# HGRN2 recurrence with the keys' logarithm in the exponents, and a new order of work at the head boundary

## The reference

```python
def hg_dir(p, z, lb):
    q = jax.nn.silu(to_heads(p[4], HG_HEADS))
    f = lbh + (1.0 - lbh) * jax.nn.sigmoid(to_heads(z, HG_HEADS).astype(jnp.float32))
    return q, 1.0 - f, to_heads(p[7], HG_HEADS), jnp.log(f)
...
b = jnp.cumsum(la, axis=2)
scores = jnp.einsum('bhtsd,bhsd->bhts', qc[:, :, :, None, :] * decay, kc)
new_state = (jnp.exp(b_end[:, :, 0, :])[..., None] * state
             + jnp.einsum('bhsd,bhsv->bhdv', kc * jnp.exp(b_end - b), vc))
```

## Time and profile before

| | |
|---|---|
| median of three runs | 2730.33 us |
| the profiled execution's own time, its span | 2731.74 us, 2729.8 us |
| PE, DVE, ACT, POOL busy over the span | 2571.3, 2054.5, 1455.5, 542.8 us |
| mean granted clock of TensorE | 0.975 of full |
| PE busy in 262 to 296 us (boundary after head 0) | 22.8 of 34 us |
| PE busy in 424 to 467 us (boundary after head 2) | 25.9 of 43 us |
| PE busy in 513 to 2730 us (all later stages) | 2121.7 of 2217 us |

### The profile page before, as it was taken

How to read it: one execution, slowest core, us unless ns; L and a number is a source line. 1 busy time by engine, 2 the same in 40 slices (tenths; PEclk the granted TensorE clock), 3 DMA queues, 4 the chain that set the end, 5 groups by cost and what they waited for, 6 DMA issues and landing times.

```text
span 2729.8 us, 45966 instructions
## 1 busy us (share of the span) xinstructions
PE 2571.3 (94%) x16329; PEld 2201.9 (81%) x16330; DVE 2054.5 (75%) x2515; ACT 1455.5 (53%) x1648; POOL 542.8 (20%) x423
## 2 busy tenths in 40 slices
PE   7998987999897999999999999999999999999995
PEld 3896766777886788877887979899989897898885
DVE  5437788545677896999879788766686778968786
ACT  5446665213443664777647565644454456645554
POOL 0035565200023211122121111111111212112111
PEclk9999988999997999999999999999999999999998
DMA  7121111442244996999969788766586678968793
GB/s 290 39 88 37 30 42 57 160 165 93 89 88 133 346 380 212 382 358 356 318 234 364 266 300 278 272 224 208 191 304 209 236 262 313 354 206 293 266 318 134
DMA packets 274965, 607.07 MB, mean 222 GB/s; under 512 B 21837, under 2 KB 52981, under 8 KB 273761
## 3 DMA queue, kind: packets, MB, share of 16 engines
q1 hardware_dynamic: 254496, 562.41, 57.7%
q0 software_dynamic: 20384, 43.51, 7.0%
HBM read 582.87 MB, written 46.97 MB: 231 GB/s over the span
## 4 chain that ended last, share of the span: by engine, by line
PE 36%; issue 11%; DVE 9%; ACT 5%; DMA 4%; SPq 1%; DVEq 1%; POOL 1%; ACTq 0%; POOLq 0%
PE e_acc L2609 7%; PE e_acc L2612 7%; PE e_acc L2610 7%; PE e_acc L2582 4%; PE e_acc L2584 4%; PE e_acc L2583 4%; DVE e_slot_r L2765 3%; ACT whi L2693 3%; DMA list_now<-lists 3%; SPq L2341 1%; PE e_tb L2551 1%; DVE yo L2851 1%; DVE e_alo L2774 1%; DVE e_glu L2827 1%; DMA slot<-in_w 1%
## 5 line engine op out<-in xcount | busy, mean ns | idle before, releaser
L2693 ACT ACTIVATE whi<-e_slot 128x2048 fp32r<-128x2048 f32 x296 | 561.5, 1914 | 395.2 <-PE e_acc L2612 327.0
L2765 DVE TENSOR_TENSOR e_slot_r<-e_slot,whi 128x2048 fp32r<-128x2048 f32 x296 | 674.9, 2287 | 114.2 <-ACT whi L2693 114.2
L2609 PE MATMUL e_acc<-e_xhi,whi 128*128 128x256 f32 x1664 | 398.9, 282 | 4.5 <-ACT e_xhi L2697 4.5
L2693 ACT ACTIVATE whi<-slot 128x2048 fp32r<-128x2048 f32 x148 | 283.2, 1913 | 180.5 <-PE e_acc L2584 180.2
L2765 DVE TENSOR_TENSOR slot_r<-slot,whi 128x2048 fp32r<-128x2048 f32 x151 | 344.3, 2282 | 24.4 <-ACT whi L2693 21.8
L2582 PE MATMUL e_acc<-whi,e_ahi 128*128 128x512 f32 x800 | 320.3, 400 | 4.3 <-DVE e_glu L2827 4.3
L2609 PEld LDWEIGHTS e_acc<-e_xhi,whi 128*128 128x128 f32 x1664 | 313.2, 188 | 7.6 <-ACT e_xhi L2697 7.6
L2584 PE MATMUL e_acc<-whi,e_alo 128*128 128x512 f32 x800 | 313.3, 392 | 0.0
L2583 PE MATMUL e_acc<-e_slot_r,e_ahi 128*128 128x512 f32 x800 | 311.4, 389 | 0.0
L2509 POOL DMA_INDIRECT sum<-yo,e_idx_now x48 | 118.5, 2470 | 949.7 <-issue 505.9
L2582 PE MATMUL e_acc<-whi,e_xhi 128*128 128x512 f32 x768 | 304.4, 396 | 1.3 <-DVE e_slot_r L2765 1.1
(11 more groups left out here) (449 smaller groups left out, 4993.3 us busy)
## 6 DMA issues: line engine op xcount, KB each, us to landing
e_slot<-in_w SPq DMA_DIRECT2D x296, 1024.0 KB, 7.6
slot<-in_w SPq DMA_DIRECT2D x151, 1024.0 KB
rv<-in_w_ada SPq DMA_DIRECT2D x32, 512.0 KB, 5.4
slot<-in_w_in SPq DMA_DIRECT2D x9, 1024.0 KB, 9.7
wa<-in_w_ada SPq DMA_DIRECT2D x8, 1024.0 KB, 17.1
slot<-in_w_in SPq DMA_DIRECT2D x12, 512.0 KB, 4.4
xt<-in_x SPq DMA_DIRECT2D x8, 512.0 KB, 14.8
slot<-in_w_out SPq DMA_DIRECT2D x4, 1024.0 KB, 14.2
```

Source lines behind the costliest of these rows:

```text
L2609: pe.matmul(out[:, c, :], whi[i % RING][:, w], xhi[:, kk, :], start=first, stop=False, skip_group_check=True)
L2693: act.activation(whi[i % RING][:], raw[i % PIECES][:], ACT.Copy).then_inc(S["whi_made"], 1)
L2765: v.tensor_tensor(wlo[i % PIECES][:], raw[i % PIECES][:], whi[i % RING][:].bitcast(F32), ALU.subtract).then_inc(S["wlo_made"], 1)
```

## The change

The keys enter as logarithms. ACT takes the sigmoid of `-z`, so that `keyA`, `keyB` hold the key without its factor; `gate_logs` has the gate as one minus factor times that; `key_logs` then turns them in place into the key's logarithm, and DVE's `keys` adds or subtracts the running sums. After that an exponential alone yields the decayed key (`key_decays`) and the key side of every level, so `decayed_keys` and the two key multiplications per level are gone. `sum_keys` forms the plain sum of both directions' keys before the logarithm, into `key_sum`.

POOL makes the same 24 differences for each half, in another order: six query and six key ones of the forward direction, `roots` of the head before between, then twelve of the backward direction.

At the boundary PE has the two gate groups of head `h + 2` behind the first transpose group. The transposes use `h_tb`, and only group 4 uses `h_po` (`turn_bank`); the next head's transposed keys are copied by DVE instead of ACT (head 0's still by ACT). On DVE the copies follow `finish`, the backward scans stand behind `keys(h + 1, 0)`, and the decayed queries are made last.

```diff
...
-        scan = t.sb("h_scan", [P, HN])
+        scan = t.sb("h_scan", [P, PAIR])
+        key_sum = t.sb("h_key_sum", [P, SEQ])
...
-        wk = t.sb("h_wk", [P, NL + 1, HN])
+        wk = t.sb("h_wk", [P, NL, HN])
...
+        def turn_bank(n):
+
+            return tb[n == 4]
+
...
             def turn_keys(h, n):
                 d, g = divmod(n, 3)
-                pe.wait_ge(S["dec_ready"], 6 * h + 2 * d + 2)
+                pe.wait_ge(S["kdec_ready"], 2 * h + d + 1)
                 if n == 0:
                     pe.wait_ge(S["states"], 2 * (LT + 1) * h)
-                if n == 1:
+                if n == 4:
                     pe.wait_ge(S["o_ready"], LT * h)
-                pe.wait_ge(S["ktok_ready"], 6 * h + max(0, n - 1))
+                pe.wait_ge(S["ktok_ready"], 6 * h + (0, 1, 2, 3, 3, 4)[n])
                 for i in range(min(4, NT - 4 * g)):
                     c = 4 * g + i
-                    tt = pe.transpose(tb[n % 2][:, i * P:(i + 1) * P], kdec[d][:, c * P:(c + 1) * P], ident[:])
+                    tt = pe.transpose(turn_bank(n)[:, i * P:(i + 1) * P], kdec[d][:, c * P:(c + 1) * P], ident[:])
...
-                    pe.wait_ge(S["ktok_ready"], 6 * h + n + 1)
+                    pe.wait_ge(S["ktok_ready"], 6 * h + (6 if n == 4 else n + 1))
...
+                    pe.wait_ge(S["key_sums"], 2 * h + half + 1)
+                    pe.wait_ge(S["lev_exp"], 2 * NL * (2 * h + half + 1))
                     pe.wait_ge(S["lev_ready"], 2 * h + half + 1)
-                pe.matmul(out[:, 0:P], wk[:, NL, i * P:(i + 1) * P], q[:, j * P:(j + 1) * P], start=True, stop=True)
+                pe.matmul(out[:, 0:P], key_sum[:, j * P:(j + 1) * P], q[:, j * P:(j + 1) * P], start=True, stop=True)
...
                     for n in range(6):
                         turn_keys(h + 1, n)
+                        if n == 0 and h + 2 < HEADS:
+                            gates_of_keys(h + 2, 0)
+                            gates_of_keys(h + 2, 1)
                     updates(h + 1)
-                    if h + 2 < HEADS:
-                        gates_of_keys(h + 2, 0)
-                        gates_of_keys(h + 2, 1)
-                    else:
+                    if h + 2 == HEADS:
                         for x in range(EARLY_FIRST):
                             early_rows(x)
...
-            def logs(h):
+            def key_sigmoids(h):
                 for d in range(2):
                     act.wait_ge(S["z_copied"], 6 * h + 3 * d + 3)
                     for x, _ in key_pieces(h, d):
-                        act.activation(x, x, ACT.Sigmoid).then_inc(S["z_sig"], 1)
+                        act.activation(x, x, ACT.Sigmoid, scale=-1.0).then_inc(S["z_sig"], 1)
+
...
-                        act.activation(ahead[:, :, 1:STEP] if d else to, tiles(x) if d else x, ACT.Ln, scale=bound[:, h, d, 1:2], bias=bound[:, h, d, 0:1]).then_inc(S["logf"], 1)
-
...
+                        act.activation(ahead[:, :, 1:STEP] if d else to, tiles(x) if d else x, ACT.Ln, scale=bound[:, h, d, 2:3], bias=offset[:, 0:1]).then_inc(S["logf"], 1)
+
+            def key_logs(h, half):
+                act.wait_ge(S["key_sums"], 2 * h + half + 1)
+                act.wait_ge(S["logf"], 4 * h + 4)
+                for d in range(2):
+                    x = key_pieces(h, d)[half][0]
+                    act.activation(x, x, ACT.Ln, scale=bound[:, h, d, 1:2], bias=offset[:, 1:2]).then_inc(S["key_logs"], 1)
+
+            def key_decays(h, d):
+                act.wait_ge(S["keys_ready"], 4 * h + 2 * d + 2)
+                if d:
+                    act.wait_ge(S["gate_part"], h)
+                    act.wait_ge(S["turned"], 6 * h)
+                    for x, part in key_pieces(h, 1):
+                        k = act.activation(kdec[1][:, part], x, ACT.Exp)
+                else:
+                    act.wait_ge(S["u_done"], 6 * h)
+                    for (x, part), (cum, _) in zip(key_pieces(h, 0), cum_pieces(h)):
+                        for i, to in enumerate(range(part.start, part.stop, P)):
+                            k = act.activation(kdec[0][:, to:to + P], tiles(x)[:, i], ACT.Exp, bias=tiles(cum)[:, i, P - 1:P])
+                k.then_inc(S["kdec_ready"], 1)
...
-                        first_level(h, half)
+                        first_level(h, half, "queries")
+                        first_level(h, half, "keys")
                         continue
-                    act.wait_ge(S["lev_sub"], DIFF * h + half * DIFF // 2 + 4 * l)
-                    for x in (wk, wq):
+                    done = DIFF * h + half * DIFF // 2 + 2 * (NL - 1) + 2 * l
+                    for x, n in ((wq, done - 1), (wk, done)):
+                        act.wait_ge(S["lev_sub"], n)
                         act.activation(x[:, l, :], x[:, l, :], ACT.Exp).then_inc(S["lev_exp"], 1)
...
-                    logs(h + 1)
-                    key_decays(h + 1)
+                    key_sigmoids(h + 1)
+                    gate_logs(h + 1)
+                    key_logs(h + 1, 0)
+                    if h + 2 < HEADS:
+                        high_chunk(3 * h + 6)
+                    key_logs(h + 1, 1)
                     query_sig(h + 1, 0)
+                    key_decays(h + 1, 0)
                 elif EARLY > EARLY_FIRST + 3:
                     early_rows(EARLY - 1)
                 roots(h, 1)
                 if more:
                     query_sig(h + 1, 1)
-                    if h + 2 < HEADS:
-                        high_chunk(3 * h + 6)
-                    query_decays(h + 1)
+                    first_level(h + 1, 0, "queries")
+                    key_decays(h + 1, 1)
+                    first_level(h + 1, 0, "keys")
                     totals(h + 1)
-                    for n in range(6):
-                        turned_keys(h + 1, n)
-                        levels(h + 1, 0, ((), (0,), (), (1,), (), (2,))[n])
+                    levels(h + 1, 0, range(1, 4))
                     if h + 2 == HEADS:
                         high_early(0)
                         high_early(1)
-                    levels(h + 1, 0, range(3, NL))
+                    levels(h + 1, 0, range(4, NL))
+                    query_decays(h + 1)
                     gate_sig(h + 1)
...
+                    if of == "q":
+                        out, x, y, op = (q4[:, :, :, 0], mb, bwd[:, :, :, 0], ALU.subtract) if d else (q4[:, :, :, 1], fwd[:, :, :, 1], mf, ALU.subtract)
+                    else:
+                        out, x, y, op = (k4[:, :, :, 1], k1[:, :, :, 1], mb, ALU.subtract) if d else (k4[:, :, :, 0], k0[:, :, :, 0], mf, ALU.add)
+                    g.tensor_tensor(out, x, y, op).then_inc(S["lev_sub"], 1)
+
+                g.wait_ge(S["cumulated"], 6 * h + 3)
+                for l in range(1, NL):
+                    difference(l, "q", 0)
+                g.wait_ge(S["keys_ready"], 4 * h + 2)
+                for l in range(1, NL):
+                    difference(l, "k", 0)
+                if roots_of is not None:
+                    roots(roots_of, 1)
+                g.wait_ge(S["cumulated"], 6 * h + 6)
+                for l in range(1, NL):
+                    difference(l, "q", 1)
+                    if l == 1:
+                        g.wait_ge(S["keys_ready"], 4 * h + 4)
+                    difference(l, "k", 1)
...
+            def sum_keys(h, half):
+                v.wait_ge(S["z_sig"], 4 * h + 4)
+                if h:
+                    v.wait_ge(S["s_done"], LT * (h - 1) + (half + 1) * HT)
+                to = key_sum[:, half * HN:(half + 1) * HN]
+                k0, k1 = (latent_key(h, d, half) for d in range(2))
+                v.tensor_scalar(to, k0, bound[:, h, 0, 1:2], None, ALU.mult).then_inc(S["summed"], 1)
+                v.wait_ge(S["summed"], 2 * h + half + 1)
+                v.scalar_tensor_tensor(to, k1, bound[:, h, 1, 1:2], to, ALU.mult, ALU.add).then_inc(S["key_sums"], 1)
+
             def keys(h, d):
-                v.wait_ge(S["logf"], 4 * h + 2 * d + 2)
-                for x, _ in key_pieces(h, d):
-                    v.tensor_scalar(x, x, bound[:, h, d, 2:3], bound[:, h, d, 1:2], ALU.mult, ALU.add).then_inc(S["keys_ready"], 1)
+                v.wait_ge(S["cumulated"], 6 * h + 3 * d + 3)
+                for half, (x, _) in enumerate(key_pieces(h, d)):
+                    v.wait_ge(S["key_logs"], 4 * h + 2 * half + d + 1)
+                    if d:
+                        k = v.tensor_tensor(tiles(x), tiles(x), ahead_pieces(h)[half][0][:, :, 0:P], ALU.add)
+                    else:
+                        k = v.tensor_tensor(x, x, cum_pieces(h)[half][0], ALU.subtract)
+                    k.then_inc(S["keys_ready"], 1)
...
             def level(h, half, l):
-                lo, hl = half * HN, LEVELS[l]
...
+                lo = half * HN
                 if l == 0:
...
-                    v.tensor_tensor(wk[:, NL, :], k0, k1, ALU.add).then_inc(S["lev_sum"], 1)
...
```

(54 more changed lines are left out.)

128 lines of the change are left out of this document (60 added, 68 removed).

## The result

The changed kernel takes 2738.66 us (median of eight runs, 2734.72 to 2741.99) against 2730.0 us of the kernel before in the same measurement: ratio 1.003, interval 1.0021 to 1.0039. It is slower by 8.7 us, where 8.5 us of gain were forecast. Its profiled execution has a span of 2737.5 us against 2729.8. Of those 7.7 us the stage `hgrn2` holds 5.4: the next stage's transposes begin at 518.76 instead of 513.32 us. The other 2.3 us lie behind it, where no instruction is different; there the profiled kernels of this study took between 2211 and 2223 us, so I read it as scatter.

A forecast was written before the change was run, and what follows sets the result against it. PE bounds the heads, so three boundaries and head 0's prelude decide, with DVE ending the last wait at the first two boundaries. 2.5 - 2.0 - 9.0 = -8.5 us, against the median 2730.33 given as 2722.0 us; range 2713 to 2730.

The forecast's parts named there:

- Prelude +2.5: Head 0's prelude: under the new bank rule PE waits 1.1 and 1.4 us for ACT's copies; bounds 0 and +3.
- Inside the head: 0: Keys in logarithms cost nothing inside a head, since PE works 46.02 of 47 us there and covers the other engines.
- A sign of being wrong that the prediction names: A first transpose later than now by over 1 us relative to the head's start: DVE's chain into it was mispriced.
- -1.0 at the first two boundaries: After heads 0 and 1: PE idles less early, but DVE ends the last wait; -1.0 us each, bounds +0.5 and -3.5.
- cover the wait for `finish`: Boundaries after heads 0 and 1: two gate groups of 8.6 us behind the first transpose group fill PE's wait for `finish`.
- -9 at the third: After head 2: updates end 4.4 us earlier, early rows wait 4.3 instead of 9.34 us; bounds -6.5 and -10.5.
- The rule weighed against the trace: VectorE and GpSimd share an SBUF port exclusively: all ten scans pay, 4.2 us at each of two boundaries; the sum took about half.
- it stays under the gate groups: At two boundaries the scans' extra time beside GpSimd is hidden behind PE's gate groups.
- R2: Slower, chance 0.08: after a 4.39 us wait gate groups run at the lower clock, 8.6 us more at two boundaries; 2739.0 us.
- a clock below 0.9 in the gate groups: Sign in the changed kernel's profile that would show the prediction wrong and point to R2.
- R3: Larger gain, chance 0.14: GpSimd finishes before the levels; -3.5 twice, -10.5, +2.0, given as -15 us, 2715.3 us.

The follow-up runs named there:

- Run 8: Kernel of Run 1 with the sixth `pick` of a head ahead of the forward scans on VectorE; stage end 499.70 us against 501.78.
- Run 1: Changed kernel with both gate groups of head h+2 back behind the updates; 2718.9 us, ratio 0.9957 to the kernel before, stage end 501.78 us.
- run 12: Run 1 plus two banks for head 0, the pick ahead, GpSimd's key differences behind the scans, its gate product behind the decayed queries; 2710.97 us, ratio 0.9934.
- run 7: Kernel of Run 1 with head 0's transposes using two banks in turn again; stage end 501.85 us against 501.78.

## Why the prediction was wrong, point by point

**Prelude +2.5: right.** Two waits, 1.12 and 1.08 us; head 0's scores come 2.02 us later (rows L707 from ACT above, against the earlier trace rows).

**"Inside the head: 0": wrong.** I left out that `pick` now stands behind key sums, forward scans and `middles`. The output behind it waits 1.6 us in each of three heads, where it waited 0.3. I had covered it with "PE works 46.02 of 47 us", but `pick` is one of PE's releasers; full busy time says only that nothing was late before. Run 8 prices these three waits at some 3 us in all, lower clock behind them included. The larger part of what the stretches out to T0 lost (3.5 and 2.4 us) is not the pick's: the clock of 0.50 between 299.97 and 306.20 us follows the wait of 3.94 us ahead of the scores, which the boundary left behind. Run 1 has the same pick and takes 48.38 us against 47.75 before and 51.20 here. A sign of being wrong that the prediction names did show here: from head 0's first scores to the next T0 it is 53.6 us against 51.9 before, over 1 us more.

**"-1.0 at the first two boundaries": wrong, and this is the step that failed.** I let the gate groups end at T0 + 10.6 us and said they "cover the wait for `finish`". They end at T0 + 12.9: the first takes 3.1, then PE waits 2.2 us (3.2 at the second boundary) for `queries`, and the second takes 7.2 us at a mean clock of 0.76 instead of 5.6. And there was no wait for `finish` left to cover: by the new bank rule the second transpose group doesn't use `h_po`, and in run 1 it waits 5.5 us for VectorE's copy. Into these 5.5 us went 8.6 us of work, 2.2 of waiting and 1.6 of lower clock, so T1 comes 6.8 us later than in run 1, at the second boundary 7.7. Even at full clock and without the wait 3.1 us would be too much. I had seen that the updates end later, and let it pass because no gate groups follow; but VectorE needs the updates, and it stood 6.85 us for T1:

```profile
279.68 0.69 DVE L1270 COPY h_ktok<-h_tb 128x512 f32<-128x512 f32 x1 [6.85 <-PE h_tb L707]
```

So the chain that ends the last wait, copies, states, levels, states, decayed queries, started with PE's delay in it. From T1 on my sum was nearly right (T1 to out 21.4 us forecast, 20.93 measured). The end is at T0 + 33.9 instead of 32.0. Run 1 undoes the placement and gets 29.5.

How much of the miss is this step: 13.9 us lie between the forecast of -8.5 and the +5.4 at the stage end, 4.8 of them at these two boundaries, 7.0 in the three stretches that lead up to the boundaries, and 2.2 at the third boundary. In run 1, with the groups in their old place, the stage ends 11.5 us and the whole time is 9.8 us below the kernel before, so without this step the gain would have been the forecast one or a little more.

**"-9 at the third": right in kind, too large.** -6.75 us. The early rows wait 4.55 us, forecast 4.3. The updates end later than forecast (T0 + 17.2 against 14.7), since T1 waits 4.99 us for a copy that VectorE makes only behind the scans and keys:

```profile
442.14 1.09 PE L707 MATMUL h_tb<-ident,h_kdec 128*128 128x128 f32 x4 [4.99 <-DVE h_ktok L1270]
...
458.24 0.77 PE L692 MATMUL h_pj<-h_early,uhi 128*128 128x512 f32 x1 [4.55 <-DVE slot_r L1200]
```

**The rule weighed against the trace: right.** The backward scans beside GpSimd take 4.59 us for six instead of 2.00, four scans beside nothing stay at 1.34: 2.6 us, against some 2.1 in the sum and 4.2 by the rule for all ten. What I did not do was let it count: I wrote that "it stays under the gate groups", while `queries`, behind those scans, is what the second group waits for. By the rule of the Trainium skill ("SBUF — State Buffer", section "Who interferes with whom") an engine holds the shared port exclusively; the traces agree, with 2.50 against 5.20 and 2.36 against 4.52 us.

**The rivals.** R2 gave 2739.0 us, and the time is 2738.66, but that it meets it so closely is luck. Its condition, a wait inside the gate groups of 4.39 us, was not met (2.2 and 3.2); the lower level came all the same, and cost 1.6 us in the group, not 8.6. It cost more at a place that R2 did not name: behind the waits of 3.94 and 5.92 us ahead of the scores. There 6.2 us behind the first output ran at 0.50 in head 1, and 6.6 us at 0.57 in head 2, which by these figures is some 3 us in each (an estimate). The rest is VectorE standing for T1 and the waits for `pick`. The sign named for it, a clock below 0.9 in the gate groups, did show: 0.86 from 266.50 to 279.04 us, 1.00 in the first group and 0.76 in the second. That R2 had 0.08 was my error: I had worked out a wait of "under 2 us" and tied the lower level to one of 4.39, and it came behind 2.2. R3's parts add up to -15.5 us, not the -15 written there; nothing hangs on it.

## What to carry to other kernels

Before filling a wait with work, check that the wait is still there, and compare lengths: what is longer than the wait, its own waits included, delays whoever stands behind it, and an engine that had slack before may be the one that ends the chain. A stretch at 98% busy is not a cover for a later releaser; list what PE waits for with margins, the picks among them. Where VectorE's products and GpSimd share a stretch, move the one with slack by a semaphore. Here the four small edits of run 12, two of them of this kind, one copy moved ahead and the old place of the gate groups make a kernel of 2708.57 us, 0.85% below the kernel before and some 30 us below the change.

## What the runs showed that I had not expected

Three products of VectorE beside a row of GpSimd's took 7.13 us in one execution (start 420.18) and 3.40 in another of nearly the same kernel. In the first, VectorE's first product took 5.93 us and was not done until GpSimd's row, eight products in that time, had ended at 425.56; the other two took 0.68 each. In the second, the two engines alternate: VectorE's products took 1.14 to 1.26 us and GpSimd's beside them 1.10 to 1.18 instead of 0.67. What decides between the two stays open. And a wait of 1.6 us of PE can be followed by the lower clock level in one execution and not in another: behind it `queries` took 5.6 us in run 1 (clock 1.00 from 255.04 to 261.81 us) and 7.2 in run 7 (0.80 from 252.80 to 261.17) on the same instructions.
